# Two transformer blocks on one core: the end of the convolution ordered by token tile

## The reference

```python
def conformer_conv(h, w_pw1, b_pw1, w_dw, b_dw, ln_g, ln_b, w_pw2, b_pw2):
    u = h @ w_pw1 + b_pw1
    a, g = jnp.split(u, 2, axis=-1)
    u = a * jax.nn.sigmoid(g)
    u = depthwise_conv(u, w_dw) + b_dw
    u = jax.nn.silu(layer_norm(u, ln_g, ln_b))
    return u @ w_pw2 + b_pw2
...
        x = x + rms_norm(m, g[1])
        h = rms_norm(x, g[2])
        x = x + rms_norm(squared_relu_mlp(h, mlp_w1[i], mlp_w2[i]), g[3])
```

## Time and profile before

| | us |
|---|---|
| median of 3 runs | 904.07 |
| lowest, highest | 901.78, 904.19 |
| the profiled execution | 897.32 |
| its span, first to last instruction | 895.5 |
| TensorE busy in the span | 882.4 |
| VectorE, ScalarE, GpSimd busy | 690.6, 290.7, 293.7 |

### The profile page before, as it was taken

The page is one execution under the profiler, slowest core; times in us unless marked ns, Lnnn a source line. Parts: engine busy times, 40 slices in busy tenths (PEclk is TensorE's granted clock), DMA queues, the critical chain, the costliest instruction groups (busy, mean ns, idle before and its releaser), DMA issues.

```text
span 895.5 us, 12926 instructions
## 1 busy us (share of the span) xinstructions
PE 882.4 (99%) x4851; PEld 742.6 (83%) x4851; DVE 690.6 (77%) x731; ACT 290.7 (32%) x568; POOL 293.7 (33%) x204
## 2 busy tenths in 40 slices
PE   9999999999999999999999999999999999999997
PEld 7987798888887787688888888888767988888885
DVE  6799888777777775889777777779578887777775
ACT  6638271111112501354111111454585541111112
POOL 2330123444434332213444443232142323333331
PEclk9999999999999999999999999999999999999999
DMA  8960636555568265216655555376143366555541
GB/s 278 343 232 1 235 100 232 189 190 190 197 221 298 82 204 187 95 52 236 213 194 193 193 198 192 104 262 198 38 189 102 105 238 215 187 187 187 187 164 47
DMA packets 82263, 160.23 MB, mean 179 GB/s; under 512 B 5080, under 2 KB 40426, under 8 KB 82224
## 3 DMA queue, kind: packets, MB, share of 16 engines
q1 hardware_dynamic: 82208, 159.69, 52.1%
q10 hardware_dynamic: 16, 0.00, 0.0%
HBM read 158.63 MB, written 1.05 MB: 178 GB/s over the span
## 4 chain that ended last, share of the span: by engine, by line
PE 91%; DMA 2%; DVE 2%; ACT 2%; POOL 1%; issue 1%; SPq 0%; DVEq 0%; POOLq 0%; ACTq 0%
PE ps L2163 88%; PE ps L2167 3%; DMA raw<-in_odd_w_pw 2%; DMA raw<-in_even_w_in 1%; ACT arena L1662 1%; POOL w_hi L636 0%; ACT arena L1850 0%; DVE w_lo L861 0%; POOL st L675 0%; DVE x_res L954 0%; DVE arena L1496 0%; POOL st L674 0%; DVE nrm L964 0%; ACT arena L2067 0%; DVE st L1203 0%
## 5 line engine op out<-in xcount | busy, mean ns | idle before, releaser
L861 DVE TENSOR_TENSOR w_lo<-raw,w_hi 128x2048 fp32r<-128x2048 f32 (+2 forms) x134 | 310.7, 2342 | 38.9 <-POOL w_hi L842 21.8
L2163 PE MATMUL ps<-act_hl,w_hi 128*128 128x512 f32 (+1 forms) x1088 | 241.2, 367 | 0.8 <-POOL w_hi L658 0.4
L2163 PEld LDWEIGHTS ps<-act_hl,w_hi 128*128 128x128 f32 x1088 | 182.4, 189 | 30.2 <-issue 1.0
L2163 PE MATMUL ps<-w_hi,act_hl 128*128 128x512 f32 (+3 forms) x656 | 181.0, 382 | 1.1 <-DVE w_lo L861 0.8
L2163 PE MATMUL ps<-w_hi,hl 128*128 128x512 f32 (+1 forms) x648 | 178.3, 388 | 0.0
L651 POOL TENSOR_SCALAR w_hi<-raw 128x2048 fp32r<-128x2048 f32 x48 | 119.0, 2479 | 149.6 <-PE ps L2163 135.2
L2163 PEld LDWEIGHTS ps<-w_hi,act_hl 128*128 128x128 f32 x656 | 118.6, 188 | 25.1 <-issue 3.4
L2163 PEld LDWEIGHTS ps<-w_hi,hl 128*128 128x128 f32 x648 | 119.2, 188 | 23.2
L2163 PEld LDWEIGHTS ps<-act_hl,w_lo 128*128 128x128 f32 x960 | 129.2, 191 | 8.2
L2163 PE MATMUL ps<-act_hl,w_lo 128*128 128x256 f32 x960 | 132.3, 283 | 0.0
L2163 PE MATMUL ps<-w_lo,act_hl 128*128 128x512 f32 (+1 forms) x328 | 104.3, 378 | 0.0
(11 more groups left out here) (241 smaller groups left out, 821.3 us busy)
## 6 DMA issues: line engine op xcount, KB each, us to landing
raw<-in_mlp_w SPq DMA_DIRECT2D x64, 1024.0 KB, 5.2
raw<-in_w_gate SPq DMA_DIRECT2D x22, 512.0 KB, 3.9
raw<-in_w_up SPq DMA_DIRECT2D x22, 512.0 KB, 4.8
raw<-in_w_down SPq DMA_DIRECT2D x11, 1024.0 KB, 4.9
raw<-in_odd_w_pw SPq DMA_DIRECT2D x16, 512.0 KB, 5.8
raw<-in_w_in SPq DMA_DIRECT2D x8, 1024.0 KB, 6.2
raw<-in_even_w_in SPq DMA_DIRECT2D x4, 1024.0 KB, 12.1
raw<-in_even_w_out SPq DMA_DIRECT2D x4, 1024.0 KB, 5.8
```

The source lines that it names most:

```text
L861: tt(w_lo[slot_of(n)][:, 0:w], raw[slot_of(n)][:, 0:w], w_hi[slot_of(n)][:, 0:w].bitcast(F32), ALU.subtract).then_inc(S("w_split"), pieces ...
L2163: return pe.matmul(o, l, r, start=start, stop=stop, skip_group_check=True)
```

## The change

Inside `inverse(b)` only tile 0's products stay. Tile 1's products of all four blocks follow in one row behind `inverse(3)`; for this `zz` gets four buffers, in the place of constants that are used up, and the wait for an old buffer goes. The narrow products of the two tiles, in alternation before, stand apart.

The rest is ordered by tile: tile 0's statistics come first, its norm is done by VectorE and its eight transposes follow tile 1's inverse products; tile 1's statistics stand on VectorE behind tile 0's first silu, its whole norm is on ScalarE (two halves of 512), and its transposes stand between pw2 products of tile 0. `keep_warm` is not called here any more. The channel groups become six, each of one tile, so that the scaling works on 128 columns and not 256. In pw2 the first piece of tile 1 comes after the first two pieces of tile 0. `gains_product(1, 5)` waits for `ln_shift` and no longer for the last silu; `pre_1` and one of `both_gains` get other places; in `boundary_later(3, ...)` `post_gain(0)` stands in front of `lo` of mlp1's first piece. The numbers of matmuls for the inverse, of transposes and of pw2 products stay the same.

```diff
-        zz = [AR(1536 * i, 2, BLOCKS, T) for i in range(2)]
+        zz = [AR(at, 2, BLOCKS, T) for at in (0, 1536, 4608, 6144)]
...
-        eb = AR(7152, 8, T)
+        eb = AR(2048, 8, T)
...
-        post_1, pre_1 = AR(4608, D), AR(7168, D)
-        both_gains = (gain[0][:, :], AR(8200, D), AR(5632, D), AR(8192, D))
+        post_1 = AR(4608, D)
+        pre_1 = (AR(7168, D), AR(9216, D), AR(7168, D), AR(7168, D))
+        both_gains = (gain[0][:, :], AR(8192, D), AR(5632, D), AR(8192, D))
...
-        Z_GROUPS = ((0, 1), (1, 1), (2, 2), (4, 2), (6, 2))
+        Z_GROUPS = ((0, 0, 2), (0, 2, 2), (1, 0, 2), (0, 4, 4), (1, 2, 2), (1, 4, 4))
...
-                gp.wait_ge(S("silu"), len(Z_GROUPS))
+                gp.wait_ge(S("ln_shift"), 1)
                 gains_product(1, 5)
...
                     g, at, base = norms[0], SCALE_LATER.index(s), ssqs[0]
-                    pre_tile_1(g + 1)
-                    lo_until(last + 1)
-                    post_gain(0)
+                    pre_tile_1(at, g + 1)
+                    if s == 3:
+                        post_gain(0)
+                        lo_until(last + 1)
+                    else:
+                        lo_until(last + 1)
+                        post_gain(0)
                     post_add_pre(s, 0, g + 1)
...
-                            if b >= 2:
-                                dve.wait_ge(S("inv"), 2 * (b - 2) + 2)
...
-                            ins = tt(zz[b % 2][:, j, blks, :], spec, filt, ALU.mult)
+                            ins = tt(zz[b][:, j, blks, :], spec, filt, ALU.mult)
...
+                row_stats(0, 1)
+                moments(0)
+                dve.wait_ge(S("ln_rstd"), 1)
+                layer_norm(0, 0)
+                layer_norm(0, 1)
+                z_odd(0, 1)
+                z_odd(0, 3)
+                silu(0)
                 row_stats(1, 0)
-                for m in range(M):
-                    row_stats(m, 1)
-                    dve.bn_aggr(mv[:, m, :], bns[:, m, :, :]).then_inc(S("ln_stats"), 1)
...
-
-                dve.wait_ge(S("ln_rstd"), 1)
-                layer_norm(0, 0, 512).then_inc(S("normed"), 1)
+                row_stats(1, 1)
+                z_low(0)
+                moments(1)
+                silu(1)
+                z_low(1)
+                z_odd(0, 5)
+                z_odd(0, 7)
                 dve.wait_ge(S("ln_rstd"), 2)
                 tsc(ln_shift, mv[:, 1, 0:1], rstd[:, 1:2], -1.0, ALU.mult, ALU.mult).then_inc(S("ln_shift"), 1)
-                layer_norm(0, 512, D).then_inc(S("normed"), 1)
-
...
-                z_odd(1)
-                dve.wait_ge(S("normed_1"), 2)
-                layer_norm(1, 768, D).then_inc(S("normed_last"), 1)
-                z_odd(3)
-                silu(0)
-                silu(1)
-                z_low(0)
+                z_odd(1, 1)
+                z_odd(1, 3)
                 silu(2)
-                z_low(1)
-                z_odd(5)
                 z_low(2)
                 silu(3)
-                z_odd(7)
                 z_low(3)
                 silu(4)
                 z_low(4)
+                z_odd(1, 5)
+                z_odd(1, 7)
+                silu(5)
+                z_low(5)
                 lo_until(FIRST["pw2"] + 3)
                 boundary_later(3, FIRST["mlp1"] - 1)
                 mlp(FIRST["mlp1"], 1)
...
+                z_even(0, 0)
+                z_tanh(0)
+                z_even(0, 2)
+                z_high(0)
+                z_tanh(1)
+                z_high(1)
+                z_even(0, 4)
+                z_even(0, 6)
                 act.wait_ge(S("ln_shift"), 1)
-                for h in (slice(0, 512), slice(512, 768)):
+                for h in (slice(0, 512), slice(512, D)):
                     f(nrm[:, 1, h], tall_out(ACC, 1)[:, h], ACT.Identity, bias=ln_shift, scale=rstd[:, 1:2])\
                         .then_inc(S("normed_1"), 1)
-
...
-                z_even(0)
-                z_tanh(0)
-                z_even(2)
-                z_tanh(1)
-                z_high(0)
+                z_even(1, 0)
                 z_tanh(2)
-                z_high(1)
-                z_even(4)
+                z_even(1, 2)
                 z_high(2)
                 z_tanh(3)
-                z_even(6)
                 z_high(3)
                 z_tanh(4)
                 z_high(4)
+                z_even(1, 4)
+                z_even(1, 6)
+                z_tanh(5)
+                z_high(5)
...
-                def turn_normed():
-
-                    for k in range(KD):
-                        for m in range(M):
-                            if k == 0:
-                                keep_warm(SPEC + 1, 10 if m == 0 else 4)
-                            if m == 0:
-                                pe.wait_ge(S("normed"), normed[0] + k // 4 + 1)
-                            elif k < 6:
-                                pe.wait_ge(S("normed_1"), k // 4 + 1)
-                            else:
-                                pe.wait_ge(S("normed_last"), 1)
-                            if m == 1 and k in (4, 6):
-                                for b in (range(3) if k == 4 else (3,)):
-                                    mm(ps[:, ACC + b, :], sel[:, b % 2, :], bias_pw2, True, False)
-                            if m == 0 and k >= 4:
-                                pe.wait_ge(S("z_odd" if k % 2 else "z"), k // 2 - 1)
-                            ins = turn(z_bank(k)[:, m * P:(m + 1) * P], nrm[:, m, k * P:(k + 1) * P])
-                        ins.then_inc(S("z_turned"), 1)
-                    normed[0] += 2
+                def turn_z(m, j):
+
+                    if m == 0:
+                        normed[0] += 1
+                        pe.wait_ge(S("normed"), normed[0])
+                    else:
+                        pe.wait_ge(S("normed_1"), j + 1)
+                        pe.wait_ge(S("z"), 2 * j + 2)
+                        pe.wait_ge(S("z_odd"), 2 * j + 2)
+                    for k in range(4 * j, 4 * j + 4):
+                        ins = turn(z_bank(m, k), nrm[:, m, k * P:(k + 1) * P])
+                    ins.then_inc(S("z_turned"), 1)
...
+                def direct(b, m):
+
+                    q, at = b // 2, T * (b % 2)
+                    for j in range(2):
+                        ins = mm(ps[:, ACC + 2 * m + q, at:at + T], inv_t[:, 2 * m + j, :], zz[b][:, j, m, :], False, True)
+                    return ins
+
+                def middle(b, m):
+
+                    q, at, half = b // 2, T * (b % 2), (slice(64, P), slice(0, 64))[m]
+                    for j in range(2):
+                        ins = mm(ps[half, ACC + 2 * m + q, at:at + T], inv_t[:, 2 * MIDDLE + j, half], zz[b][:, j, MIDDLE, :],
+                                 False, True)
+                    return ins
...
                     pe.wait_ge(S("zz"), 2 * b + 1)
-                    direct(0)
+                    direct(b, 0)
                     pe.wait_ge(S("zz"), 2 * b + 2)
-                    for j in range(2):
-                        for m, half in enumerate((slice(64, P), slice(0, 64))):
-                            ins = mm(ps[half, ACC + 2 * m + q, at:at + T], inv_t[:, 2 * MIDDLE + j, half],
-                                     zz[b % 2][:, j, MIDDLE, :], False, True)
-                            if j and m == 0:
-                                ins.then_inc(S("inv"), 1)
-                    direct(1).then_inc(S("inv"), 1)
+                    ins = middle(b, 0)
+                    if b % 2:
+                        ins.then_inc(S("inv"), 1)
...
                 inverse(3)
-                turn_normed()
-
-                tall(FIRST["pw2"], ACC, act_hl, 0, False, False, 2, 1024, k_waits=(lows[0] + 1, lows[0] + 2))
-                tall_by_tile(FIRST["pw2"] + 1, [(act_hl, 2), (act_hl, 4), (act_hl, 6)],
-                             waits=[("act_lo", lows[0] + j) for j in (3, 4, 5)], turn_bank=TURN_BANK[3])
-                lows[0] += 5
+                for b in range(4):
+                    direct(b, 1)
+                    ins = middle(b, 1)
+                    if b % 2:
+                        ins.then_inc(S("inv"), 1)
+                turn_z(0, 0)
+                turn_z(0, 1)
+                pw2_bias(0)
+
+                def pw2(j, m, half=None, free=False):
+
+                    return tall(FIRST["pw2"] + j, ACC, act_hl, 2 * j, False, j == 3, 2, 1024, tiles=(m,), free=free, half=half)
+
+                need_lows(lows[0] + 1)
+                pw2(0, 0)
+                turn_z(1, 0)
+                need_lows(lows[0] + 2)
+                pw2(1, 0)
+                turn_z(1, 1)
+                pw2_bias(1)
+                need_lows(lows[0] + 3)
+                pw2(0, 1, free=True)
+                need_lows(lows[0] + 4)
+                pw2(2, 0)
+                pw2(3, 0).then_inc(S("tile_out"), 1)
+                for h in range(2):
+                    for j in range(1, 4):
```

(7 more changed lines are left out.)

87 lines of the change are left out of this document (47 added, 40 removed).

## The result

| | changed | before |
|---|---|---|
| median | 910.93 us, 6 runs (906.68 to 911.69) | 902.91 us, 6 runs (900.53 to 904.19) |
| profiled execution, its span | 906.68, 904.9 | 897.32, 895.5 |

The ratio is 1.009 [1.0065, 1.0116]: the change makes the kernel slower by 8 us, where +4.1 was forecast. The sign was right and 910.93 lies just inside the range, near its top of 911.0, which stood for a loss of clock; the size of the forecast itself, 908.2, is off by a factor of two.

The account below looks back on a forecast made before the run. TensorE was taken to bound the kernel. Filler -3.0, products +4.9, idling +2.05 and starts +0.15 made +4.1 us, so 901.4 for the profiled execution; with 6.75 for the median, 908.2, range 904.0 to 911.0.

Parts of the forecast that it names:

- Point 2: Inverse transforms split by token tile: both halves take 4.16 us against 2.94, for four transforms +4.9 us.
- the first rival: In the split inverses, narrow products cost nothing alone: 903.3 to 904.7 us; chance 0.20 together with a shorter chain.
- Point 3: Tail of tile 1's inverse products: takes 8.32 us, ends at 368.6, and hides the first tile's norm.
- Point 4: From the turned tile to pw2: a chain of 3.3 us, pw2 starts near 372.5, TensorE idles 2.5 us.
- Point 5: Inside pw2: 0.45 us wait for tile 1's norm; the gains product costs nothing or up to 1 us.
- Point 6: Next boundary, post_gain(0) ahead of the split of mlp1's first piece: taken as 0, at most +0.9 us.
- The local sum: Around the change: pw2 starts 2.2 us later, then 0.45 + 1.5 more, all else as before: +4.1 us.
- Point 1: Filler before the transposes removed: 14 x 0.216 = -3.0 us, nothing else depends on it, some becomes waiting.
- the fall: Rival: TensorE's clock falls once at the unfilled wait before pw2, +5.8 us, 909.9; chance 0.12 together with a late load.
- the 6.75: Whole kernel: the median of runs lies 6.75 us above the profiled execution, taken as the same after the change.
- The first tile's chain: Rival: the reordered first tile reaches pw2 without the wait, -2.5 us, 905.7; chance 0.20 together with cheap narrow products.
- the late load: Rival: the load released by mlp1's first piece is needed at once, 3 us added; chance 0.12 together with the clock.

Follow-up runs that it names:

- e3: The kernel before, with tile 1's full-width products put between the two tiles' narrow products in each inverse, filler kept; 904.57 us, ratio 1.0021 to before.
- e1: The changed kernel with both tiles' narrow products in alternation again inside each inverse; 903.04 us, ratio 1.0009 to the kernel before.
- e4: The changed kernel with z_low(0) in front of tile 1's two statistics on VectorE; 905.91 us, ratio 1.0041 to the kernel before.
- e11: The changed kernel with ten filler matmuls in the wait before pw2, a second time; 904.79 us, ratio 1.0049 to the kernel before.
- e13: The changed kernel unaltered, its third measurement; 907.48 us, ratio 1.0080 to the kernel before.
- e7: The changed kernel with ten filler matmuls in the wait before pw2; 904.05 us, ratio 1.0039 to the kernel before.
- e6: The changed kernel unaltered, measured again; 907.94 us, ratio 1.0064 to the kernel before.
- the repeats: The two further measurements of the unaltered changed kernel against the kernel before: 907.94 against 901.56 us and 907.48 against 901.82 us.
- the first comparison: The original measurement of the changed kernel against the kernel before: 910.93 against 902.91 us, ratio 1.009.
- e8: The kernel before with 30 filler matmuls, not 10, in front of the first transpose; 906.16 us, ratio 1.0040 to before.
- e9: The changed kernel with narrow products paired, tile 1's first statistics moved into tile 0's root wait, seven fillers before pw2's bias products; 901.56 us, ratio 0.9994 to before.
- e10: The changed kernel with ten filler matmuls in front of the tail of tile 1's products; 910.03 us, ratio 1.0108 to the kernel before.
- e2: The kernel before without its 14 filler matmuls; 903.65 us, ratio 1.0017 to before.

## Why the prediction was right and where it failed

**Point 2, right.** The split costs 4.8 where 4.9 stood (e3, clean executions; 4.6 in its timeline), and taking it back returns the whole loss (e1). With it falls the first rival: a lone narrow product takes the full step of 0.216. Of e3's 1.15 a transform, 0.86 are the four lost steps and 0.29 the second change between wide and narrow. The Trainium skill, "TensorEngine Tiling (Array Packing)", Key Properties, says both, that different tiles work in parallel and that a change of mode drains the engine, without a price; the trace agrees.

**Point 3, right.** Tile 1's products end at 369.29, or 368.4 without the 0.87 of the late start, forecast 368.6; the tail, whose first product starts at 361.01, takes 8.3 as said.

**Point 4, nearly.** From the last bias product's start to pw2's first product are 2.77 us, so with one step of 0.22 taken off TensorE idles 2.55 (the profile's own figure is 2.37), forecast 2.5; pw2 starts at 373.22, or 372.4 without the 0.87, forecast 372.5. That the two statistics stand in this chain is right (e4 takes 0.9 of the wait away), but the gain is not to be had, since the other tile pays.

**Point 5, a miss of 0.45 that didn't matter.** The wait for tile 1's norm stays away: at 376.11 TensorE finds it done. It appears as 1.34 only in e4. The gains product (2.41 us) ran at 375.32 beside no VectorE step, so its bound of 1 us stayed unused.

**Point 6, in its range.** I took 0 and bounded it by 0.9. The profile's idle time is 0.43; from start to start the eight transposes with the wait between them take 1.44 where they took 0.79, so it costs 0.65. The mechanism is one that I had only named as work beside it. The changed kernel's timeline of VectorE:

```profile
390.12 2.29 DVE L872 TENSOR_TENSOR w_lo<-raw,w_hi 128x2048 fp32r<-128x2048 f32 x1
393.26 0.75 DVE L987 SCALAR_TENSOR_TENSOR x_res<-nrm,st,x_res 128x512 f32<-128x512 f32 x1 [0.85 <-POOL st L686]
```

And its timeline of GpSimd:

```profile
390.18 2.40 POOL L685 TENSOR_SCALAR st<-st 128x1 f32<-128x1 f32 x1 [4.90 <-ACT arena L1686]
392.66 0.56 POOL L686 TENSOR_TENSOR st<-st 128x1 f32<-128x1 f32 x1
```

Since `post_gain(0)` now stands ahead of `lo`, the small step of the root on GpSimd meets `lo` and takes 2.40 us for 128 elements. In the kernel before, the same one came after `lo` and took 0.30:

```profile
385.73 0.30 POOL L674 TENSOR_SCALAR st<-st 128x1 f32<-128x1 f32 x1 [5.73 <-ACT arena L1662]
```

**The local sum, partly luck.** That 4.3 came out where 4.1 stood rests on misses that cancel: pw2 starts 2.0 later where 2.2 stood, the 0.45 of point 5 never came, and 0.65 came at point 6 where 0 stood.

**Point 1, the step that failed.** "14 x 0.216 = -3.0 us. Nothing else depends on it." The clock depends on it. I priced the fall as a rival with a chance of 0.12 beside the sum, once and only right behind the wait, where it is a term on top of the sum: the filler covered that wait. Putting it back into the changed kernel's wait returns 2.7 to 3.9 us (e11 against e13, e7 against e6). Against the kernel before the clock's share is smaller in the repeats, 1.9 and 2.3, and 4.1 in the first comparison, since most executions of before lose clock too. That was to be seen: I carried the 6.75 between the median and the profiled execution over as a constant, and by the line about 5 of it is lost clock, a mean near 0.993 against 0.999. For the repeats the account closes by the median clocks, 0.994 and 0.996: 902.1 + 6 x 0.9 = 907.5 (measured 907.48 and 907.94), and 897.9 + 4 x 0.9 = 901.5 for before (901.56 and 901.82). In the first comparison the mean clocks are mostly 0.990 or 0.991 in the changed kernel, and 902.1 + 10 x 0.9 = 911.1 fits the 910.93. The Trainium skill, "TensorE: Matmul & The Clock Gate", "Why this matters for your kernels", tells to avoid idle gaps between bursts. Its row speaks of gaps longer than these; a fall follows in four profiles of eight all the same, and in four it doesn't. I gave the warning too little since no row of before showed a fall, but in before the filler filled the wait, so its rows could not speak.

**The other rivals.** The first tile's chain was not shorter than forecast (pw2 at 372.4 against 372.5), and the late load cost nothing, since the shift stays as it is behind mlp1's first product.

**What stays open.** The profile shows the place of a fall for one execution per kernel. Most of the loss that I can place lies in the second block's attention, at 660 to 678, also in kernels with filler (e8, e9, e11). About one fall per execution, 1.7 us, can be put to the wait before pw2. Seven of the eight profiles without filler in their waits have 6.8 us at the lower level in that attention, three of them (the first of the changed kernel, e1 and e10) without any fall at the convolution's end, and of the six with filler one has as much. So the filler and the clock go together, and a fall right behind the wait is not the whole way from one to the other. What that way is, and why the first comparison lost more than the repeats, isn't settled. For `e1_pair`, without a clean execution, the lost clock is seen in the runs but its profile has no fall at the end of the convolution.

## What to carry to other kernels

Work that is moved to hide a wait must cost nothing by being moved: here 8.3 us of products covered a norm of about 3, and setting them apart broke pairs that ran side by side, at 1.2 us a transform. With the pairs kept, 3.5 us of products covered the norm but for 0.25, at no cost (e1). Before filler is counted as saved time, ask what its place would be without it: a wait that it covered and perhaps a clock that it held, and neither shows in the trace of the kernel that has it. Where the time of an execution follows its mean granted clock, fit or select by clock first and compare the work at equal clock; medians alone mixed two effects of opposite sign (e2, e3).

## What the runs showed of the hardware

- Narrow products of one half that follow each other, with nothing for the other half between, take the full 0.216 us step; alternating halves run in pairs, a whole transform of 16 instructions in 2.94 us against 4.1.
- Inside the span, its first 20 and last 6 us aside, every stretch at the lower clock level lasted 3.4 or 6.8 us; ten of the 14 profiles have one. Behind waits of 2.4 us, or of 1.85 and 0.87 close together, at the convolution's end TensorE went on at the lower level in four of six profiles; with filler in the wait in none of six.
- 0.001 of mean granted clock is 0.90 us of this kernel.
- A GpSimd step on 128x1 values took 2.39 to 2.40 us beside VectorE's 2.29 us `w_lo<-raw,w_hi`, in all nine profiles with `post_gain(0)` in front, and 0.30 to 0.45 elsewhere. The Trainium skill, "GPSIMD Engine Reference", 1. Specifications, names contention with VectorE instructions that have two SBUF inputs; `w_lo` is one, and the trace agrees.
